# Hybrid attention and RWKV trunk: low-rank mix two chunks earlier, one ScalarE table set for the attentions, gates read back sooner, x in four parts

## What is computed

```python
h = rms_norm(x, norm_g[l])
p = h @ w_in[l]                                    # 2048 x 12480
p_sb, p_mla, p_rw, p_gate = split_cols(p, (SB_COLS, MLA_COLS, RW_COLS, GATE_COLS))
y_sb  = stick_breaking_attention(sq, sk, sv) * silu(sg)          # 4 heads of 128
y_mla = chunk_causal_softmax_attention(q, k, v_m) * silu(mg)     # 8 heads, low-rank q and kv
rw_main = rw_main + rw_mu[l] * (prev - rw_main)                  # prev: one row earlier
rr, rk, rv, wd, ad = split_cols(rw_main, (RW_WIDTH,) * 3 + (DECAY_LORA, ICL_LORA))
y_rw  = rwkv7_mixer(rr, rk, rv, wd, ad, ...) * silu(rg)          # 8 heads of 64
g_sb, g_mla, g_rw = split_cols(sigmoid(p_gate), (D_MODEL,) * 3)
merged = g_sb * (y_sb @ w_br_sb[l]) + g_mla * (y_mla @ w_br_mla[l]) + g_rw * (y_rw @ w_br_rw[l])
x = x + merged @ w_out[l]
```

## Time and profile before

| | |
|---|---|
| median of 3 runs | 1809.63 us (1808.51 to 1810.19) |
| the profiled execution's own time | 1811.34 us |
| its span | 1809.6 us |
| PE, DVE, ACT, POOL busy | 98%, 59%, 49%, 8% |
| TensorE's mean granted clock | 0.997 |
| DMA | 333.10 MB, mean 184 GB/s |

### The profile page before, as it was taken

How to read it: one execution, slowest core, us unless ns; L and a number is a source line. 1 busy time by engine, 2 the same in 40 slices (tenths; PEclk the granted TensorE clock), 3 DMA queues, 4 the chain that set the end, 5 groups by cost and what they waited for, 6 DMA issues and landing times.

```text
span 1809.6 us, 22320 instructions
## 1 busy us (share of the span) xinstructions
PE 1778.5 (98%) x8914; PEld 1499.1 (83%) x8914; DVE 1073.4 (59%) x1388; ACT 880.2 (49%) x1235; POOL 138.6 (8%) x158
## 2 busy tenths in 40 slices
PE   7999999999999999999999999999999999999998
PEld 7778888888888888788888788888888888787887
DVE  4677464554766645676545774654556666466753
ACT  6454443434455566555454545434344555755542
POOL 1001020210000000100010010211100000000000
PEclk9999999999999999999999999999999999999999
DMA  8865554545655555876677655545465555458654
GB/s 262 233 194 170 158 170 145 163 149 155 187 178 152 168 152 163 287 258 196 187 249 210 183 163 152 166 150 174 134 179 183 163 155 168 138 189 303 237 187 154
DMA packets 176863, 333.10 MB, mean 184 GB/s; under 512 B 20492, under 2 KB 33210, under 8 KB 176120
## 3 DMA queue, kind: packets, MB, share of 16 engines
q1 hardware_dynamic: 167784, 297.67, 53.9%
q0 software_dynamic: 8976, 34.01, 5.3%
HBM read 311.46 MB, written 16.78 MB: 181 GB/s over the span
## 4 chain that ended last, share of the span: by engine, by line
PE 88%; DMA 4%; DVE 4%; ACT 3%; issue 1%; SPq 0%; ACTq 0%; DVEq 0%
PE D L580 74%; PE B L580 11%; DMA ring<-in_w_in 2%; DMA ring<-in_w_br_rw 2%; ACT arena L895 1%; DVE w_lo L1225 1%; ACT w_hi L895 1%; DVE arena L1225 1%; ACT L895 1%; PE B L636 1%; DVE xy L1225 0%; PE B L652 0%; PE B L875 0%; DVE gev L1263 0%; PE B L746 0%
## 5 line engine op out<-in xcount | busy, mean ns | idle before, releaser
L1225 DVE TENSOR_TENSOR w_lo<-ring,w_hi 128x1024 fp32r<-128x1024 f32 (+3 forms) x560 | 661.3, 1195 | 444.0 <-ACT w_hi L895 436.1
L895 ACT ACTIVATE w_hi<-ring 128x1024 fp32r<-128x1024 f32 (+3 forms) x560 | 572.9, 1037 | 375.7 <-PE D L580 285.9
L580 PE MATMUL D<-w_hi,ht_hi 128*128 128x512 f32 (+2 forms) x1728 | 692.2, 401 | 7.3 <-DVE w_lo L1225 7.3
L580 PE MATMUL D<-w_hi,ht_lo 128*128 128x512 f32 (+2 forms) x1728 | 668.5, 387 | 0.0
L580 PE MATMUL D<-w_lo,ht_hi 128*128 128x512 f32 (+2 forms) x1728 | 667.1, 386 | 0.0
L580 PEld LDWEIGHTS D<-w_hi,ht_hi 128*128 128x128 f32 x1728 | 326.8, 189 | 71.1 <-DVE w_lo L1225 7.3
L580 PEld LDWEIGHTS D<-w_hi,ht_lo 128*128 128x128 f32 x1728 | 326.0, 189 | 67.0
L580 PEld LDWEIGHTS D<-w_lo,ht_hi 128*128 128x128 f32 x1728 | 327.0, 189 | 57.3 <-issue 0.5
L580 PEld LDWEIGHTS B<-arena 128*128 128x128 f32 (+3 forms) x1568 | 205.3, 190 | 24.4 <-issue 7.3
L580 PE MATMUL B<-arena 128*128 128x128 f32 (+5 forms) x1568 | 220.3, 293 | 1.2 <-DVE arena L1399 0.8
L895 ACT ACTIVATE arena<-B 128x512 f32<-128x512 f32 (+4 forms) x168 | 81.0, 491 | 286.9 <-PE B L580 229.2
(11 more groups left out here) (138 smaller groups left out, 1275.9 us busy)
## 6 DMA issues: line engine op xcount, KB each, us to landing
ring<-in_w_in SPq DMA_DIRECT2D x368, 512.0 KB, 4.0
ring<-in_w_out SPq DMA_DIRECT2D x64, 512.0 KB, 4.7
ring<-in_w_br_mla SPq DMA_DIRECT2D x32, 512.0 KB, 4.9
gate_spill<-gev POOLq DMA_DIRECT2D x24, 512.0 KB, 4.2
arena<-gate_spill POOLq DMA_DIRECT2D x24, 512.0 KB, 4.8
ring<-in_mla_w_ukv SPq DMA_DIRECT2D x16, 512.0 KB, 4.2
ring<-in_w_br_rw SPq DMA_DIRECT2D x16, 512.0 KB, 5.8
ring<-in_w_br_sb SPq DMA_DIRECT2D x16, 512.0 KB, 5.1
```

Source lines behind the costliest of these rows:

```text
L580: return nc.tensor.matmul(o, a, b, start=start, stop=stop, skip_group_check=True)
L895: return nc.scalar.activation(o, i, fn, **kw)
L1225: return v.tensor_tensor(o, a, b, op)
```

## The change

Four edits. DVE's mix of the low-rank inputs moves from chunk 16 to chunk 14. Behind the Sigmoids of rg and mg0 ACT preloads the set that holds both Exp and Ln. The first gates are read back when the last latent attention head is through DVE (`ml_dve` 24), not when sg's silu product is. x is read back in four parts of 512 columns, each behind one of the gates 6 to 9, with a semaphore each, and DVE waits for the part of its block.

```diff
-        x_in, x_new = sem("x_back"), sem("x_new")
+        x_in, x_new = [sem(f"x_back{j}") for j in range(4)], sem("x_new")
...
-                pool.wait_ge(silu_dve[l], 8)
+                pool.wait_ge(ml_dve, 24 * l + 24)
                 for n in range(12):
                     if n >= 3:
                         pool.wait_ge(gate_used[l], n - 2)
                     gate = spill[(2 - n % 3) * 4 + n // 3].rearrange("(h p) c -> p h c", p=P)
                     pool.dma_start(GT[:, n % 3, :, :], gate
                                    ).then_inc(gate_in[n % 3][l], 16)
-                    if n == 2:
-                        pool.wait_ge(br_pe[l], 8)
-                        pool.wait_ge(x_settled[l], 4)
-                        pool.dma_start(xy[:], (out if l else x)[0].rearrange("(h p) d -> p h d", p=P)
-                                       ).then_inc(x_in[l], 16)
+                    if 6 <= n < 10:
+                        j = n - 6
+                        if j == 0:
+                            pool.wait_ge(br_pe[l], 8)
+                            pool.wait_ge(x_settled[l], 4)
+                        c = slice(j * 512, (j + 1) * 512)
+                        pool.dma_start(xy[:, :, c], (out if l else x)[0, :, c].rearrange("(h p) d -> p h d", p=P)
+                                       ).then_inc(x_in[j][l], 16)
...
                         last.then_inc(silu_sig[l], 1)
+                        if n < 2:
+                            act.preload_act_table_set("natural_log_exp_and_others")
                         continue
...
-                    if j == 0:
-                        dve.wait_ge(x_in[l], 16)
+                    dve.wait_ge(x_in[j][l], 16)
...
-                dense_to(AT_LORA)
+                dense_to(AT_LORA - 2)
                 dve.wait_ge(mu_in[0][l], 16)
```

## The result

The changed kernel took 1789.74 us (median of 4 runs, 1788.80 to 1790.13) beside 1809.39 us for the kernel before (4 runs, 1808.51 to 1810.19). The ratio is 0.9894, 95% interval 0.9878 to 0.9909: faster by 19.7 us, 1.1%. The forecast was 1789 us, in a range of 1785 to 1798. The profiled execution took 1790.13 us, with a span of 1788.4; before, 1811.34 and 1809.6. It is 21.2 us shorter, and the prediction's sum was 21.7.

The account below looks back on a forecast made before the run. PE was taken to bound the kernel. Idle 15.3, overlap 1.3 and clock 5.1 us made 21.7 us, giving 1789.6 from the profiled 1811.3 and 1787.9 from the median; forecast 1789 us, range 1785 to 1798.

Parts of the forecast that it names:

- Bound by PE: Whole kernel: PE is busy 1778.5 of 1809.6 us, so only its standing still or running slowly can be won.
- Part 1: ACT, both stick-breaking pairs: sixteen table loads fewer; waits of 3.6 and 2.1 us go, preloads cost 0.
- The `w_lo` term: First stick-breaking pair, both layers: `w_lo` comes early enough that PE's stall of 1.81 us goes, 3.6 us together.
- Part 2: Low-rank stage: the mix ends 2.4 us before PE asks, so 3.9 us of waits go, 0 added.
- Part 3: Branch stage: early gates and x in four parts remove PE's stalls of 2.4 and 3.3 us, 5.7 together.
- the rule on turns: DMA queues: equal turns would keep the weights 187 of 374 GB/s; the sum went by the trace's bytes instead.
- rival A: Branch stall stays or moves to the next bank change; gives back 7.7 us: 1797 us; chance 0.09.
- the margin: Weight loads beside the parts of x: 9.3 us at worst, stall begins at some 11.5, so 2.2 us in hand.
- The clock: Three stretches at 1.2 instead of 2.4 GHz right behind stalls go with them: 1.7 us each, 5.1 together.
- B: The clock falls stay, elsewhere; gives back 5.1 us: 1794.7 us; chance 0.07.
- C: No change: each removed wait is followed by one for a weight transfer; 1810 us; chance 0.03.
- D: Slower: gate and part of x together starve the weights at every merge-stage bank change; 1839 us; chance 0.03.

Follow-up runs that it names:

- Part 1 alone: The kernel before with only the two table preloads per layer: 1800.40 us, ratio 0.9962.
- Part 2 or Part 3 alone: Two runs on the kernel before: only the mix two chunks earlier, 1802.65 us; only the early gates and x in four parts, 1801.02 us.
- the first set: The runs made for the result: the changed kernel 1789.74 us beside the kernel before at 1809.39 us, 4 runs each.
- the last set: The runs of the last four experiments, with the kernel before run among them: median 1804.71 us, 7 runs.

## Why the prediction was right, and where it was not

**Bound by PE: right.** All but 0.5 of the 21.2 us between the two profiled executions came from PE's waits, the overlap lost at them, and its clock. ACT's busy time fell by 880.2 - 860.5 = 19.7 us too, the same as the time, but that is chance: it is the sixteen loads of 1.28 (20.5), and by the waits Part 1 was worth about a third of the whole.

**Part 1: right.** Both steps of its working have their row: 3.83 us earlier in the first pair; in the second the wait is gone with the preload, and returns at its exact 2.1 us without it. The 1.2 us in hand behind mg0 are 1.5 by the run with two more loads, and behind rg, where I had no row, 1.1. The `w_lo` term was set at 3.6 and gave 2.6, though both waits of 1.8 us are gone: the waits for `w_lo` at the starts of the layers grew from 3.3 to 4.4 us, so 4.7 are left where 7.3 - 3.6 = 3.7 were expected. Nothing in the change touches those, and the group varies by as much on its own: 7.3 to 8.3 us in the profiled executions that keep the first pair's waits, 3.9 to 6.1 in those without.

**Part 2: right, 3.9.** In the two profiles that compare them the second chunk of the move neither brought nor cost anything but margin: 1.9 us in hand instead of 0.4. The wait itself was long in the execution that I read: 2.5 to 3.6 us in the six others that still have it.

**Part 3: right in its sum, 5.7, flawed in its reasons.** The step that failed is the reading of the rule on turns. I took equal turns as equal bytes, 187 GB/s for the weights, and wrote that the trace does not agree. But the Trainium skill, DMA: Bandwidth & Descriptors, section Queues, rings and completion order, speaks of a packet at a time, and the packets of the two queues differ in size. Where all queues have work, the counts of the profile's packets agree with the rule: to 2% in the first two windows above, and within 6% with the early gates, with x whole at the later place, and with three queues. That the packets which the profile lists are those of the page is taken for granted here. The earlier trace rows had it in part: 660 packets to 506 in a window whose start belongs to the gates alone, and 3.49 MB to 1.00. Rightly read, the rule speaks for cutting x into shorter rows, and rival A has no rule behind it. The expectation for the four parts at once shows the same flaw: it held the amount for the cause, and the run refuted it.

The second flaw is the margin. 9.3 us was forecast as the worst weight load against a threshold of 11.5. It was 10.9 and 11.3. The 11.5 itself is confirmed for the old place of the reads, and if it holds at the new one, the 2.2 us in hand were 0.6 and 0.2: what was mis-sized is the load beside a gate and a part, 9.3 for 11.3. The forecast held by less than it said. Third, the part was costed as one, but its edits overlap. Smaller rows alone leave 0.6 us of the stall, the early gates alone 0.5, and the later parts with the gates late none. x later alone, whole and with the gates late, was not run.

**The clock: 5.1 us, right for this execution and not as a rule.** All three falls of the earlier trace rows are gone. But which stall brings one is not fixed: with Part 1 alone two falls stood at branch stalls, with the early gates alone one at 658.2 (the first pair), with the later parts alone one at 1547.8 (the first pair of layer 1), with x on ACT's queue one at 55.2 (the mix), with Part 2 or Part 3 alone none. A stretch lasted 3.4 us each time, and began between 0.4 us before and 1.4 us behind the end of a stall. So the sum was of one execution, and this is the step of the prediction that doesn't hold in general: it put each fall down to its stall as a fixed term. The kernel before shows the falls as scatter. In its 58 later runs the time goes with the mean granted clock: the nine with 1.000 took 1803.6 to 1805.3 us, 1804.5 on average, the four with 0.997 took 1808.6 to 1810.5, the one with 0.995 took 1813.9. The changed kernel's two runs with 1.000 took 1788.8 and 1789.3. So 15 to 16 us are gained without any fall, which is the idle time and the overlap (14.3 + 1.3). The rest of the 19.7 is probably falls in the first set: its clocks are not on record, but its times, 1808.5 to 1810.2, are those that the later sets show at 0.997. The forecast of a gain near 21 came close partly by luck: the profiled execution had three falls and the first set was like it, while the last set's median (1804.71, clock 1.000) had none, and the variant that stands nearest to the changed kernel there (the mix one chunk earlier) gained 15.8. The forecast of 1789 us for the changed kernel itself doesn't rest on that luck in the same way, as it took the falls out of an execution that had them. Within a set the kernel before ranged over up to 9.5 us in 26 runs, while the changed kernel and four of its variants, four runs each, stayed within 1787.2 to 1794.2, no kernel over more than 2.7 (the one without the preload behind mg0 ranged over 4.6). Four runs show less of a scatter than 26.

**The sum.** Idle 2.6 + 2.1 + 3.9 + 5.7 = 14.3 by the waits (14.5 by the page), overlap 1.3, clock 5.1: 20.7 of the 21.2. The term that was mis-sized between these two executions is `w_lo`, by 1.0. **Rivals.** A and B did not come in the changed kernel: no D wait on `arena`, no slow stretch. B's argument, that a stall alone doesn't say when a fall comes, is right. C's fear of a next-late supplier showed only in that 1.0. D's mechanism, a gate and a part together, is real (the load of 10.9), but stopped short of its point.

## What to carry over

When one engine is busy for 98% of the span, sum its waits by group, ask of each what stands ahead of the late instruction on the engine that supplies it, and move that away by what the margin asks for. Of the three edits of the DMA part one could have been left out, either the early gates or the cutting of x. Two DMA streams that compete are compared in packets and in bytes: the one with longer packets takes more, whichever queue it is on, and shorter rows or another time both help. Choose the window so that all queues have work throughout it, or the counts mislead. The waits and the clock falls of one profiled execution are a sample, here one from the slow end: the falls stood at a different stall each time, so a prediction should carry them as a range and not as a term.

## What was unexpected of the hardware

- Packet size decides the share: 378 weight packets of 2 KB moved 0.74 MB against 372 of mostly 4 and 8 KB with 2.34 MB; with x in rows of 512 elements, 555 moved 1.07 against 553 with 2.05. With three queues at once, 114, 120 and 115 packets moved 0.93, 0.49 and 0.21 MB.
- Moving the transfer from POOL's queue to ACT's left the stall (4.6 us, longest load 13.9, time 1807.86 beside 1805.48).
- A table load takes 1.28 us wherever it stands, also three in a row (670.65, 671.93, 673.22), and the next function starts 0.01 to 0.02 behind it. The Trainium skill, ScalarE: Activation LUTs, section What ACT_TABLE_LOAD costs, adds a drain of 1380 ns to the load, 2.66 us together. These rows show no such drain.
- Table loads in the trace number 34 before and 18 after, one more each than in the order of ACT; the difference is the sixteen that were forecast.
